# Eighteen places instead of fourteen for the gathered down rows of an expert stage, on one core of a Trainium2

## The chip, the cores and the metric

The kernel runs on one core of a Trainium2 chip. The metric is the device time of one execution in microseconds (us). The kernel before took 2483.57 us, the median of three runs (2480.18 to 2490.12).

A core has four computing engines that run side by side: PE (TensorE, the matrix engine; the profile lists its weight loads apart, as PEld), DVE (VectorE), ACT (ScalarE) and POOL (GpSimd). SP (SyncE) only issues transfers here. Each engine takes its own list of instructions strictly in order, and engines wait for each other by semaphores: an instruction raises a counter when it is done, another waits until the counter has reached a value. DMA engines move data between the device memory and SBUF, the core's working memory; matmuls add up in PSUM.

## The reference

The reference is two blocks of a network on 256 tokens of width 1024, in float32. The part that the change touches is the expert layer of the first block (`peer`). For every token and each of 8 heads it finds 16 experts, takes one row of `peer_u` and one row of `peer_v` for each, and sums up:

```python
q = (xt @ w_pq).reshape(T, PEER_HEADS, 2, PEER_QDIM // 2)
s = jnp.einsum('thpd,hpnd->thpn', q, subkeys).astype(jnp.float32)
top_s, top_i = lax.top_k(s, PEER_TOPK)
...
act = jax.nn.gelu(jnp.einsum('thkd,td->thk', peer_u[eb], xb), approximate=False) * gb
return jnp.einsum('thk,thkd->td', act, peer_v[eb])
```

Both tables have 16384 rows of 1024 numbers. Which rows are wanted is known only when the scores of the token have been sorted, so the rows are gathered by index. Behind this layer come the second block's feed-forward layers and mixers, all of them dense matrix products with streamed weights.

## The kernel before, in words

The kernel is a sequence of stages; in each, every engine has its own list. The stage of interest is `peer_experts` (line 2299). The 256 tokens stand as 2 blocks of 128, one token per partition. A *job* is one head of one block (16 jobs), and each job has 16 *slots*, so there are 256 slots, called rows 0 to 255 below. For row i the engines do this:

- POOL, `gather(i)` (lines 2509 to 2524), issues two indirect DMAs: the u row of 128 tokens (128 x 1024 numbers, 0.52 MB) into one of `U_RING` = 6 places, and the v row ("down row", of the same size) into one of `V_RING` = 14 places. It does so strictly in the order u(0), v(0), u(1), v(1), and so on. Before u(i) it waits until the dot product of row i-6 is done (line 2516).
- DVE (line 2685) multiplies the u row with the tokens and sums it into one number per token, the *dot* of row i. Between the dots DVE sorts scores (`top16`) and works out which experts the next jobs use (`experts_of`) and their gates (`gates_of`), at fixed places of its list. `gates_of(2)` stands ahead of the dot of row 28.
- ACT, `weigh` (lines 2436 to 2450), turns two dots at a time into weights (a gelu, times the gate) and writes each weight on the diagonal of a 128 x 128 matrix. There are `DIAGONALS` = 8 of these matrices, so the diagonal of row i waits until PE has used that of row i-8 (line 2448).
- PE, `weighted_row(i)` (line 2361 on), multiplies that diagonal matrix with the v row in two halves, adding up in PSUM (line 2365), and raises `rows_used` by one.

What the v gather waits for is this (lines 2519 to 2524):

```python
if i >= V_RING:
    pool.wait_ge(S["rows_used"], (i - V_RING) + 1)
elif i >= EARLY_SLOT:
    pool.wait_ge(k.w.used, k.w.early + i - EARLY_SLOT + 1)
```

So rows 0 to 5 wait for nothing. The eight places of rows 6 to 13 (`v_rows_early`) first hold chunks 4 to 11 of the query weights `w_pq`, and row 6+c waits until PE has used chunk 4+c. From row 14 on, row i waits until PE has used row i-14.

The stage begins with the queries: PE computes 16 of them (`queries(n)`, query 0 still in the stage ahead), 1 to 3 from rounded and low parts of the tokens (the pair of tensors `moving_mem`, line 3659, passed as `parts`), 4 to 15 from whole numbers (line 2354). Queries 1 to 11 come ahead of `weighted_row(0)`, 12 to 15 are put between rows 8 and 15. After each query ACT copies it out (line 2425) and PE computes key scores with it (line 2342), which ACT copies out as well (line 2432). ACT's list has all of this and the exponentials of the gates (line 2418); those for `gates_of(2)` come behind the diagonals of rows 16 and 17.

At the end of the stage, block 0 is complete with row 239. ACT copies its sum (`total_out(0)`, line 2483, behind the diagonals of rows 242 and 243), PE transposes it (line 2399, ahead of row 246), DVE adds it to the residual (`add_features(0)`, line 2638) ahead of the dot of row 249. The rest follows behind row 255.

Of the kernel before, what the change touches and what calls it, by code (L numbers as in the profile page):

```python
# [25 lines left out]
D = 1024  # L26
# [9 lines left out]
PEER_HEADS, PEER_KEYS, TOPK = 8, 128, 16  # L36
# [19 lines left out]
SPLIT = 4  # L56
CHUNK = 8 * P
LEVELS = 7
X_SUM = 5
U_RING, V_RING, DIAGONALS = 6, 14, 8  # L60
EARLY_CHUNKS = 8
SPLITS_LEFT = 3

# [1977 lines left out]
def token_mixer(k, mem, mem_parts, parts):  # L2041
    with ExitStack() as ctx:
        sb = lambda name, *shape: k.sbuf(ctx, name, *shape)
        m = {"parts": parts, "spare": mem, "w_ba": sb("w_ba", KT, 8), "rows": sb("gdn_rows", 8),
             "beta": sb("beta", TB, 4), "decay": sb("decay", 3, TB, 4),
             "z": sb("z_silu", 4, T), "squares": sb("squares_and_outputs", 8, T),
             "gates": sb("gates", 16, T), "qkv": sb("qkv", 12, T)}
        m |= {"o_sb": m["squares"][:, 0:4, :], "o_gdn": m["squares"][:, 4:8, :]}
        with ExitStack() as early:
            eb = lambda name, *shape: k.sbuf(early, name, *shape)  # L2050
            m |= {"sb_qk": eb("sb_qk", 8, T), "sb_v": eb("sb_v", TB, 512),
                  "conv_in": eb("conv_in", 12, T + CONV_TAPS - 1), "mem_scale": eb("mem_scale", 2, T)}
            project_in(k, m, mem, mem_parts)
            stick_breaking(k, m)
        gdn_chunks(k, m)
        merged = k.pair(ctx, "merged", KT, T)
        project_residual(k, merged, "g_cross", parts, mem_parts, make=MergedBranches(k, ctx, m, merged))


def cross_attention(k, parts, mem_parts, subkeys):  # L2060

    with ExitStack() as ctx:
        q, kk = k.sbuf(ctx, "xq", KT, T), k.sbuf(ctx, "xk", KT, T)
        v_tok = k.sbuf(ctx, "xv", TB, D)
        project_residual(k, parts, "g_peer", mem_parts, mem_parts, tokens=k.xn, make=CrossHeads(k, ctx, q, kk, v_tok, parts, mem_parts, subkeys))
# [188 lines left out]
def peer(k, parts, subkeys, last_rows):  # L2254


    with ExitStack() as ctx:
        peer_experts(k, ctx, parts, subkeys, last_rows)
# [40 lines left out]
def peer_experts(k, ctx, parts, keys, last_rows):  # L2299

    S, stale = k.stage()
    first = k.w.taken - 1
    N, K = 2 * PEER_HEADS, TOPK
    SLOTS_ALL = JOBS * K
    EARLY_SLOT = V_RING - EARLY_CHUNKS
    SCORES_AT, FIRST, LAST_AHEAD = 2, 8, 12
    sb = lambda name, *shape, dtype=F32: k.sbuf(ctx, name, *shape, dtype=dtype)
    route = Route(k, ctx)
    q, diagonal = sb("peer_q", 2, T), keys
    totals = k.xn[:, :, :].rearrange("p n d -> p (n d)").rearrange("p (b d) -> p b d", b=TB)  # L2310
    dots = sb("expert_dots", SLOTS_ALL)
    gelus, weights = sb("expert_gelus", SLOTS_ALL), sb("expert_weights", SLOTS_ALL)
    u_rows, first_rows = sb("u_rows", U_RING, D), sb("v_rows", EARLY_SLOT, D)
    places = [first_rows[:, s, :] for s in range(EARLY_SLOT)] + [last_rows[:, c, :] for c in range(EARLY_CHUNKS)]
    v_row = lambda i: places[i % V_RING]
    x_squares = route.key_scores
    block_of = lambda i: (i // K) % TB
# [8 lines left out]
    with k.nc.Block() as block:  # L2326
        @block.sync
        def _(sp):
            clear(sp, stale)
            k.w.load_ahead(sp, first, N - RING - SPLIT + len(SPLIT_AT))  # L2330
            last = SLOTS_ALL - 1
            sp.wait_ge(k.v_ready[last % V_RING], 16 * (last // V_RING + 1))
            k.w.load_ahead(sp, first, N - SPLIT + len(SPLIT_AT))
# [173 lines left out]
        @block.gpsimd  # L2507
        def _(pool):
            def gather(i):
                index = bass.IndirectOffsetOnAxis(ap=route.experts[:, i // K, i % K:i % K + 1], axis=0)  # L2510
                if i in (0, FIRST):
                    pool.wait_ge(S["routed"], i // FIRST + 1)
                elif i % K == 0:
                    pool.wait_ge(S["routed"], i // K + 2)
                if i >= U_RING:
                    pool.wait_ge(S["dots"], i - U_RING + 1)
                pool.indirect_dma_start(out=u_rows[:, i % U_RING, :], out_offset=None, in_=k.dram["peer_u"],  # L2517
                                        in_offset=index).then_inc(k.u_ready[i % U_RING], 16)
                if i >= V_RING:
                    pool.wait_ge(S["rows_used"], (i - V_RING) + 1)  # L2520
                elif i >= EARLY_SLOT:
                    pool.wait_ge(k.w.used, k.w.early + i - EARLY_SLOT + 1)
                pool.indirect_dma_start(out=v_row(i), out_offset=None, in_=k.dram["peer_v"],  # L2523
                                        in_offset=index).then_inc(k.v_ready[i % V_RING], 16)

            for i in range(SLOTS_ALL):
                gather(i)
# [410 lines left out]
def nsa_mixer(k):  # L2938

    with ExitStack() as ctx:
        sb = lambda name, *shape: k.sbuf(ctx, name, *shape)
        m = {"q": sb("nsa_q", 4, T), "cmp_in": sb("cmp_in", 2, 2, T), "k_sw": sb("nsa_k", 2, T),
             "v_sw": sb("nsa_v", TB, 2, P), "conv": sb("conv_in2", 12, T), "w_g": sb("w_g", KT, 24),
             "gates": sb("nsa_gates", TB, 24), "cmp": sb("nsa_cmp", NSA_HEADS * TB, 32), "o": sb("nsa_o", KT, T),
             "w1": sb("cmp_w1", 2, CMP_STRIDE, P), "w2": sb("cmp_w2", 2, NSA_DIM), "pos": sb("cmp_pos", 2, CMP_STRIDE),
             "kc": sb("kc", N_CMP), "vc": sb("vc", NSA_REP, P), "parts": k.pair(ctx, "moving", KT, T)}
        project_late(k, "l0_mix_post_g_2", m["parts"], NsaHeads(k, ctx, m), banks=(6, 7, 2, 3))  # L2950
# [703 lines left out]
def build(nc, dram):  # L3654

    with ExitStack() as ctx:
        k = Kernel(nc, ctx, dram)
        with ExitStack() as until_peer:
            mem_parts = k.pair(until_peer, "moving_mem", KT, T)
            with ExitStack() as early:  # L3660
                parts, mem = k.pair(early, "moving", KT, T), k.sbuf(early, "mem", KT, T)
                load_and_norm(k, mem)
                token_mixer(k, mem, mem_parts, parts)
                subkeys = k.sbuf(until_peer, "subkeys", 2 * PEER_HEADS, PEER_KEYS, side="right")
                last_rows = k.sbuf(until_peer, "v_rows_early", EARLY_CHUNKS, D, side="right")
                k.w.early_places = [last_rows[:, c, :] for c in range(EARLY_CHUNKS)]
                cross_attention(k, parts, mem_parts, subkeys)
            peer(k, mem_parts, subkeys, last_rows)
        ffn(k, "l0_ffn1", final="g_final")
        nsa_mixer(k)  # L3670
        ffn(k, "l0_ffn2")
        ffn(k, "l1_ffn1")
        rwkv_mixer(k)
        ffn(k, "l1_ffn2")
        store_output(k)
# [113 lines left out]
```

## Time and profile before

| | |
|---|---|
| median of three runs | 2483.57 us (2480.18 to 2490.12) |
| the profiled execution | 2478.28 us, its span 2476.3 us |
| granted clock of PE, mean over the span | 0.95 |
| PE, PEld, DVE, ACT, POOL busy | 89%, 73%, 65%, 40%, 20% of the span |
| first and last gather of the expert stage | 419.56 and 1163.65 us |
| what is gathered | 268.47 MB of the 509.44 MB that all DMAs move |

The profile is of one execution; its times are counted from the start of its span. An engine's row in a timeline gives start, duration, engine, line, operation, tiles and number of instructions, and in brackets how long the engine had been idle and what ended that. The names that the profile gives to releasers are inferred: where a row says that a DMA from the start of the program (`x_residual<-in_x`) ended a wait, it was something else, and the code has to be asked. The diagonal matrices lie where the keys lay, and appear as `subkeys`.

### The profile page before, as it was taken

The page shows a single profiled execution, that of the slowest core. Times are in us where ns is not written, and L with a number is a line of the kernel's source. Part 1 is how long each engine was busy: PE and PEld are TensorE (multiplying, and loading weights), DVE is VectorE, ACT ScalarE, POOL GpSimd, SP SyncE. Part 2 cuts the span into 40 slices and gives each one's busy share as a digit, 9 for nine tenths or more (in the row PEclk, how much of TensorE's full clock was granted, in tenths as well). Part 3 has the DMA queues.
Part 4 walks back from the last instruction along what each step waited for, and adds up shares of the span by engine and source line. Part 5 has one row for each costly group of instructions (what it writes and reads, how often), then busy time and mean ns, then how long its engine had stood idle before and what let it go on. Part 6 is the DMA issues. An engine that isn't in the chain of part 4 may idle for free. (4 is left out here: it accounts for less than half of the span.)

```text
span 2476.3 us, 40698 instructions
## 1 busy us (share of the span) xinstructions
PE 2201.6 (89%) x15970; PEld 1804.3 (73%) x15970; DVE 1616.7 (65%) x3172; ACT 987.7 (40%) x1894; POOL 503.2 (20%) x532
## 2 busy tenths in 40 slices
PE   8998999897777776767999999999999898999998
PEld 7987988542222322223999997999999777888998
DVE  6676756765566566553766766766766868648666
ACT  5553544243233332322544444444543563014433
POOL 0000001566666666664100000000000000000000
PEclk9999999898898888888999999999999999999999
DMA  5530573899999999998455541555455432002653
GB/s 204 180 96 18 172 254 134 313 355 366 373 371 364 370 371 367 367 384 326 146 183 184 181 128 60 163 182 184 153 184 183 145 94 86 3 3 90 195 184 111
DMA packets 140318, 509.44 MB, mean 206 GB/s; under 512 B 15968, under 2 KB 16608, under 8 KB 139744
## 3 DMA queue, kind: packets, MB, share of 16 engines
q1 hardware_dynamic: 65824, 237.32, 29.8%
q0 software_dynamic: 73728, 268.47, 28.6%
q8 instruction: 128, 2.10, 0.3%
q10 hardware_dynamic: 576, 1.05, 0.1%
q14 instruction: 62, 0.51, 0.1%
HBM read 505.72 MB, written 1.05 MB: 205 GB/s over the span
## 5 line engine op out<-in xcount | busy, mean ns | idle before, releaser
L249 DVE TENSOR_TENSOR weights_low<-weights,weights_high 128x1024 fp32r<-128x1024 f32 x424 | 520.6, 1229 | 284.8 <-ACT weights_high L240 282.7
L240 ACT ACTIVATE weights_high<-weights 128x1024 fp32r<-128x1024 f32 x424 | 446.7, 1058 | 495.0 <-PE ps L285 382.2
L283 PE MATMUL ps<-moving_high,weights_high 128*128 128x256 f32 x2126 | 609.0, 286 | 8.7 <-DVE moving_low L1350 3.8
L285 PE MATMUL ps<-moving_high,weights_low 128*128 128x256 f32 x2126 | 602.9, 284 | 0.0
L284 PE MATMUL ps<-moving_low,weights_high 128*128 128x256 f32 x2126 | 602.9, 284 | 0.0
L2685 DVE CUSTOM_DVE_ANT_0 u_rows<-u_rows,ps 128x1024 f32<-128x1024 f32 x256 | 308.3, 1219 | 236.2 <-DMA u_rows<-in_peer_u,experts 178.0
L2365 PE MATMUL ps<-v_rows_early,subkeys 128*128 128x512 f32 x576 | 305.8, 685 | 137.8 <-issue 123.6
L283 PEld LDWEIGHTS ps<-moving_high,weights_high 128*128 128x128 f32 x2126 | 409.4, 193 | 13.0 <-issue 9.9
L284 PEld LDWEIGHTS ps<-moving_low,weights_high 128*128 128x128 f32 x2126 | 409.3, 193 | 0.2
L285 PEld LDWEIGHTS ps<-moving_high,weights_low 128*128 128x128 f32 x2126 | 409.0, 192 | 0.0
L2365 PEld LDWEIGHTS ps<-v_rows_early,subkeys 128*128 128x128 f32 x576 | 121.3, 218 | 316.1 <-issue 316.0
L2517 POOL DMA_INDIRECT u_rows<-in_peer_u,experts x256 | 241.9, 945 | 457.2 <-DVE experts L2600 372.1
L2365 PE MATMUL ps<-v_rows,subkeys 128*128 128x512 f32 x448 | 210.0, 620 | 40.6 <-issue 36.6
L2365 PEld LDWEIGHTS ps<-v_rows,subkeys 128*128 128x128 f32 x448 | 87.2, 199 | 158.2 <-issue 158.0
L2796 PE MATMUL ps<-hidden_high,weights_high 128*128 128x256 f32 x704 | 199.2, 283 | 0.0
L2796 PE MATMUL ps<-hidden_low,weights_high 128*128 128x256 f32 x704 | 199.2, 283 | 0.0
L2796 PE MATMUL ps<-hidden_high,weights_low 128*128 128x256 f32 x704 | 199.2, 283 | 0.0
L3598 POOL COPY inverse_t<-consts 128x512 f32<-128x512 f32 x8 | 4.6, 614 | 931.9 <-POOLq L3054 872.2
L2449 ACT ACTIVATE subkeys<-consts,expert_weights 128x128 f32<-128x128 f32 x256 | 89.9, 389 | 192.4 <-DMA x_residual<-in_x 136.0
L2523 POOL DMA_INDIRECT v_rows_early<-in_peer_v,experts x144 | 136.7, 949 | 90.2 <-issue 34.7
L2796 PEld LDWEIGHTS ps<-hidden_high,weights_high 128*128 128x128 f32 x704 | 135.2, 192 | 0.0
L2796 PEld LDWEIGHTS ps<-hidden_low,weights_high 128*128 128x128 f32 x704 | 135.2, 192 | 0.0
(600 smaller groups left out, 3417.6 us busy)
## 6 DMA issues: line engine op xcount, KB each, us to landing
weights<-in_l_ffn SPq DMA_DIRECT2D x264, 512.0 KB, 3.6
weights<-in_w_in SPq DMA_DIRECT2D x44, 512.0 KB, 3.7
weights<-in_l_in SPq DMA_DIRECT2D x24, 512.0 KB, 3.6
weights<-in_l_rkv SPq DMA_DIRECT2D x24, 512.0 KB, 3.5
weights<-in_w_ckv SPq DMA_DIRECT2D x16, 512.0 KB, 4.0
weights<-in_w_up_pair SPq DMA_DIRECT2D x8, 512.0 KB, 3.6
weights<-in_w_mix_out SPq DMA_DIRECT2D x8, 512.0 KB, 4.2
weights<-in_w_cq SPq DMA_DIRECT2D x8, 512.0 KB, 5.1
```

The costliest lines, as they stand in the source:

```text
L240: act.activation(self.high[:, c % SPLIT, :], self.source(c), ACT.Copy).then_inc(self.rounded, 1)
L249: v.tensor_tensor(self.low[:, c % SPLIT, :], self.source(c), self.high[:, c % SPLIT, :].bitcast(F32), ALU.subtract).then_inc(self.split, 1)
L283: pe.matmul(out, lhs.high, rhs.high, start=start, stop=False)
L284: pe.matmul(out, lhs.high, rhs.low, start=False, stop=False)
L285: return pe.matmul(out, lhs.low, rhs.high, start=False, stop=stop)
L2365: last = pe.matmul(k.ps[:, sum_bank(tb) + half, :], diagonal[:, i % DIAGONALS, :], v_row(i)[:, 512 * half:512 * half + 512], start=i < TB ...
L2449: act.activation(diagonal[:, n % DIAGONALS, :], k.const("identity"), ACT.Copy, scale=weights[:, n:n + 1])\
L2517: pool.indirect_dma_start(out=u_rows[:, i % U_RING, :], out_offset=None, in_=k.dram["peer_u"], in_offset=index).then_inc(k.u_ready[i % U_R ...
L2523: pool.indirect_dma_start(out=v_row(i), out_offset=None, in_=k.dram["peer_v"], in_offset=index).then_inc(k.v_ready[i % V_RING], 16)
L2685: v.tensor_tensor_reduce(out=row, in0=row, in1=tokens[block_of(i)], scale=1.0, scalar=0.0, op0=ALU.mult, op1=ALU.add, accum_out=dots[:, i: ...
L2796: last = pe.matmul(acc[:, o, :], w[:, o, :], m, start=f == n == 0 and o % 2 == 0, stop=f == FT - 1 and n == 2, skip_group_check=True)
L3598: pool.tensor_copy(u[:, g, :, :], over(k.const("identity"), 4)).then_inc(S["identities"], 1)
```

## The change

`V_RING` goes from 14 to 18, and four of the places (`BORROWED`) are a new tensor of the expert stage, `v_rows_in_parts`. It is the first tensor that the stage allocates, and the pair `moving_mem` is given back just ahead of the stage, so it lies where the tokens' rounded and low parts lay. To make this possible, `subkeys` and `v_rows_early` move to another scope. The four borrowed places are those of rows 6 to 9; each of these waits until PE has used chunk 3 of the query weights, the last product that reads the parts. Rows 10 to 17 wait for chunks 4 to 11, as rows 6 to 13 did, and from row 18 on row i waits until PE has used row i-18. There are 18 semaphores for landed v rows in place of 14, and SP's wait for the last of them follows the new count. Nothing else changes: the number of transfers and of instructions that compute stays.

```diff
-U_RING, V_RING, DIAGONALS = 6, 14, 8
+U_RING, V_RING, BORROWED, DIAGONALS = 6, 18, 4, 8
...
     EARLY_SLOT = V_RING - EARLY_CHUNKS
+    BORROWED_SLOT = EARLY_SLOT - BORROWED
...
+    rows_in_parts = sb("v_rows_in_parts", BORROWED, D)
...
-    u_rows, first_rows = sb("u_rows", U_RING, D), sb("v_rows", EARLY_SLOT, D)
-    places = [first_rows[:, s, :] for s in range(EARLY_SLOT)] + [last_rows[:, c, :] for c in range(EARLY_CHUNKS)]
+    u_rows, first_rows = sb("u_rows", U_RING, D), sb("v_rows", BORROWED_SLOT, D)
+    places = [first_rows[:, s, :] for s in range(BORROWED_SLOT)] + [rows_in_parts[:, s, :] for s in range(BORROWED)]
+    places += [last_rows[:, c, :] for c in range(EARLY_CHUNKS)]
...
                 elif i >= EARLY_SLOT:
                     pool.wait_ge(k.w.used, k.w.early + i - EARLY_SLOT + 1)
+                elif i >= BORROWED_SLOT:
+                    pool.wait_ge(k.w.used, first + SPLIT)
...
-        with ExitStack() as until_peer:
+        with ExitStack() as until_ffn, ExitStack() as until_peer:
...
-                subkeys = k.sbuf(until_peer, "subkeys", 2 * PEER_HEADS, PEER_KEYS, side="right")
-                last_rows = k.sbuf(until_peer, "v_rows_early", EARLY_CHUNKS, D, side="right")
+                subkeys = k.sbuf(until_ffn, "subkeys", 2 * PEER_HEADS, PEER_KEYS, side="right")
+                last_rows = k.sbuf(until_ffn, "v_rows_early", EARLY_CHUNKS, D, side="right")
...
+            until_peer.close()
             peer(k, mem_parts, subkeys, last_rows)
```

## Rows read from the trace of the kernel before

**Rows 1.** Groups of POOL's instructions, 419 to 1166 us: name, shapes, count, busy, mean ns, idle before.

```profile
L2517 POOL DMA_INDIRECT u_rows<-in_peer_u,experts x256 | 241.9, 945 | 457.2 <-DVE experts L2600 372.1 <-issue 74.6 <-DVE expert_dots L2685 10.4
```

**Rows 2.** POOL's timeline: the first gather, one row at full pace, the last gather.

```profile
419.56 1.15 POOL L2517 DMA_INDIRECT u_rows<-in_peer_u,experts  x1 [372.11 <-DVE experts L2600]
...
479.85 0.94 POOL L2523 DMA_INDIRECT v_rows<-in_peer_v,experts  x1 [0.30 <-issue]
481.09 0.94 POOL L2517 DMA_INDIRECT u_rows<-in_peer_u,experts  x1 [0.30 <-issue]
482.33 0.94 POOL L2523 DMA_INDIRECT v_rows<-in_peer_v,experts  x1 [0.30 <-issue]
...
1163.65 0.94 POOL L2523 DMA_INDIRECT v_rows<-in_peer_v,experts  x1 [0.30 <-issue]
```

**Rows 3.** Stretches: length, busy time (instructions) of five engines, PE clock, DMA share, GB/s.

```profile
443.00:470.00 27.00, 26.57 (x122) 22.00 (x121) 20.59 (x75) 11.56 (x38) 11.71 (x14) 0.94 0.74 237
535.00:1165.00 630.00, 454.06 (x906) 185.08 (x905) 361.86 (x825) 191.06 (x607) 415.59 (x440) 0.85 0.97 368
...
557.00:573.00 16.00, 11.63 (x27) 4.67 (x25) 10.80 (x20) 4.44 (x14) 12.04 (x14) 0.98 1.03 410
```

**Rows 4.** POOL's waits for v places, 535 to 1165 us: total, times, longest.

```profile
POOL v_rows L2523 <- DMA x_residual<-in_x: 26.4, 11, 4.2
POOL v_rows_early L2523 <- DMA x_residual<-in_x: 23.6, 10, 4.6
POOL v_rows L2523 <- PE ps L2365: 23.2, 15, 5.1
...
POOL v_rows_early L2523 <- PE ps L2365: 11.5, 11, 3.4
```

**Rows 5.** POOL's timeline: v(8) and v(13), waiting for query chunks, and v(17).

```profile
447.23 0.94 POOL L2523 DMA_INDIRECT v_rows_early<-in_peer_v,experts  x1 [3.88 <-PE ps L2354]
...
467.42 0.94 POOL L2523 DMA_INDIRECT v_rows_early<-in_peer_v,experts  x1 [1.72 <-PE ps L2354]
...
477.36 0.94 POOL L2523 DMA_INDIRECT v_rows<-in_peer_v,experts  x1 [0.30 <-issue]
```

**Rows 6.** DVE's timeline: the gates of job 2 and the dot of row 28; POOL's: u(34).

```profile
521.00 0.16 DVE L2629 RECIPROCAL gate_sum<-gate_sum 128x1 f32<-128x1 f32 x1 [6.42 <-ACT expert_gates L2418]
...
521.34 1.21 DVE L2685 CUSTOM_DVE_ANT_0 u_rows<-u_rows,ps 128x1024 f32<-128x1024 f32 x1
...
530.12 0.94 POOL L2517 DMA_INDIRECT u_rows<-in_peer_u,experts  x1 [0.30 <-issue]
```

**Rows 7.** PE's timeline: rows 34 to 41, and 43; then 44 to 47.

```profile
551.07 13.90 PE L2365 MATMUL ps<-v_rows_early,subkeys 128*128 128x512 f32 x32
...
568.16 1.96 PE L2365 MATMUL ps<-v_rows,subkeys 128*128 128x512 f32 x4 [1.48 <-issue]
578.94 8.91 PE L2365 MATMUL ps<-v_rows,subkeys 128*128 128x512 f32 x16 [8.82 <-issue]
```

**Rows 8.** The same moment on ACT (diagonals 44 and 45) and POOL (v(50), v(61)).

```profile
578.39 0.69 ACT L2449 ACTIVATE subkeys<-consts,expert_weights 128x128 f32<-128x128 f32 x2 [8.73 <-DMA x_residual<-in_x]
...
578.29 0.94 POOL L2523 DMA_INDIRECT v_rows_early<-in_peer_v,experts  x1 [4.65 <-DMA x_residual<-in_x]
...
609.61 0.94 POOL L2523 DMA_INDIRECT v_rows<-in_peer_v,experts  x1 [2.77 <-PE ps L2365]
```

**Rows 9.** The stage's end: PE's rows 238 to 241, ACT's copy of block 0's sum.

```profile
1126.02 7.03 PE L2365 MATMUL ps<-v_rows,subkeys 128*128 128x512 f32 x16
...
1150.40 1.08 ACT L2483 ACTIVATE x_normed<-ps 128x512 f32<-128x512 f32 x2 [16.34 <-DMA x_residual<-in_x]
```

**Rows 10.** POOL's timeline at the end: v(240), v(254), u(255); DVE's block 0 sum.

```profile
1118.71 0.94 POOL L2523 DMA_INDIRECT v_rows<-in_peer_v,experts  x1 [2.77 <-PE ps L2365]
...
1158.37 0.94 POOL L2523 DMA_INDIRECT v_rows<-in_peer_v,experts  x1 [5.14 <-PE ps L2365]
1162.41 0.94 POOL L2517 DMA_INDIRECT u_rows<-in_peer_u,experts  x1 [3.10 <-DVE expert_dots L2685]
...
1159.71 1.28 DVE L2638 TENSOR_TENSOR x_residual<-x_residual,ps 128x512 f32<-128x512 f32 x2 [14.28 <-PE ps L2399]
```

**Rows 11.** PE's last query 5 products, ACT's copy of query 5.

```profile
427.67 2.76 PE L2354 MATMUL ps<-x_normed,v_rows_early 128*128 128x256 f32 x12
...
440.93 0.38 ACT L2425 ACTIVATE peer_q<-ps 128x256 f32<-128x256 f32 x1 [7.68 <-remote]
```

## The prediction

> **What bounds the kernel now.** The change lies in one stage, so I looked first at POOL's groups and waits, then at the stretches, and last at the timelines of all engines around single waits. The stage's gathers run from 419.6 to 1163.65 us [rows 2]: 744.1 us for 256 rows, 2.91 us each. At full pace POOL issues a row's two gathers in 2.48 us (479.85 to 482.33), so POOL alone would need 635 us. A row is 1.049 MB; where the transfers run full they move 410 GB/s [rows 3], which is 2.56 us a row, 655 us in all. The stage is thus paced by its gathers, but stands 89 us above what they need. It is not lost on u places, for which POOL waited 10.4 us in the whole stage [rows 1], but on v places: 26.4 + 23.6 + 23.2 + 11.5 = 84.7 us in 47 waits between 535 and 1165 us [rows 4], of which 0.3 each is the ordinary step between instructions [rows 2], so 70.6 us. Ahead of 535 us there are waits for query chunks, 3.88 us and five of 1.7 to 2.4 [rows 5]; there the transfers fall to 237 GB/s [rows 3].
>
> This looks like an invitation to add places. Whether they help depends on why the place isn't free. The row to look at is v(50): it waits until row 36 is used, till 578.29 us [rows 8]. PE's rows 34 to 41 ran from 551.07 at 1.72 us each [rows 7], so row 36 was through at about 556.2. The count reached POOL 22 us later. ACT waited for the very same count (diagonal 44 wants row 36 used) until 578.39, and PE stood idle for 8.8 us for want of that diagonal. At the stage's end it is seen again: row 239 is through on PE at about 1129.5 (1126.02 and two rows), and ACT, which waits for it, goes on at 1150.40 [rows 9]. So in this stage PE's counts arrive late, by about 20 us, though PE had nothing to do. I read from the two timelines that it happens while the gathers keep the transfers full (410 GB/s in the stretch ahead of 573), and that the counts come once POOL has stopped issuing for a few us: 4.65 us here, 5.14 us at v(254) [rows 10]. That POOL's stop lets the counts through is an inference; the rows show only that they come together.
>
> **The change, part by part.** *Unchanged work.* 512 gathers, 256 dots, diagonals and weighted rows stay; the new tensor, the scopes and four more semaphores issue nothing. SP's wait for the last v row moves to another semaphore, for the same row. No cost: bound 0 on both sides, unless places elsewhere in SBUF move data differently, for which no row gives a reason.
>
> *The start.* Rows 6 to 9 now wait for chunk 3, which was used before query 5's last products began at 427.67 [rows 11], earlier than v(6) is issued. v(7)'s own wait, whose count came late too, I leave as it is. From 441.2 us POOL can run at 2.49 us a row until v(17), which wants chunk 11, as v(13) did: it goes out at 467.4 in place of 477.4 [rows 5], 10.0 us or four rows ahead. This lead is cut at row 34: u(34) needs the dot of row 28, which stands behind the gates of job 2; these come from ACT at 521.0, behind queries 12 to 15 and the diagonals up to row 17, a chain that no gather feeds. The dot ends at 522.5, u(34) was at 530.1 [rows 6]: lead 7.6 us, three rows. Queued behind POOL's waiting u(34) are only later gathers. The fourth row comes back where POOL next meets a v wait, since it may then run four rows further.
>
> *The steady part.* If the reading above holds, four more places let POOL run four rows further into the time in which counts are held back, once. After that POOL stops as before, for 3 to 5 us, and gets as many rows for it as before: the eight that ACT's diagonals allow PE to be ahead of the count, and the three or four that PE gets counted soon after. Now that is 11 rows from v(50) to v(61), 31.3 us [rows 8]. ACT, stopped by the ring of eight diagonals, is not helped by v places at all. So POOL keeps a lead of three to four rows, and the pace of the counts, which PE's and ACT's work follows, stays. Ends for this part: 0 if nothing but the lead remains, 67 us if all waits fall away (first rival). I take 0, by the row where ACT and POOL wait for the same count.
>
> *The end.* What is the lead worth? v(240) went out at 1118.71 [rows 10]; v(244) would in its place, and v(254), ten rows on and with no wait, at 1143.6 in place of 1158.4. Then u(255) waits for the dot of row 249, behind the sum of block 0, which DVE adds at 1159.71. That sum hangs on ACT's copy at 1150.40. POOL now stops at 1144.5; the counts came 4.9 us after its stop at 1153.2, so now at about 1149.4. ACT's copy is 1.0 us earlier, and what follows takes as long as before. So of 10 us only about 1 survives at the tail. Between 1 and 10 us I take 3, near the lower end: 1 from the tail, and 2 because in some of the twenty stretches ACT waits for dots rather than for a count, where the lead serves it.
>
> The sum: 2478.28 - 3 = 2475.3 us for the profiled execution. The median of the runs shown lies 5.3 us above it, so 2483.57 - 3 = 2480.6 us.
>
> There is one page to weigh here. The Trainium skill, "HBM Reference", Specifications, gives about 358 GB/s as the effective rate of one core; by it 268.5 MB would take about 750 us, the stage would already be at its limit, and no number of places could shorten it (estimate: 2483.6 us). The trace disagrees: 410 GB/s over 16 us, and a mean of 368 over 630 us [rows 3]. So the room is there, and this rule does not lower the chance of the rivals that gain.
>
> **The rivals.** *All v waits fall away.* If counts come late by some 20 us whatever POOL does, four places (10 us) cover every single wait of up to 5.1 us, and the transfers become the bound: from v(36) to v(255), 219 rows, 560 us at 2.56 in place of 627. That is -67, about 2416 us. For it: the waits are short and one by one. Against: ACT's ring of eight diagonals waits for the same counts and would stop PE, and in the rows at hand counts came after stops.
>
> *Fewer stops.* Each stop buys 16 rows in place of 12, since the longer lead lets PE work off more when counts flow. The waits of 70.6 us shrink by a quarter, 17.6, and 10 us of lead last to the end: -28, about 2456 us. For it: between stops POOL is what limits. Against: just after a stop PE works without a gap (rows 44 to 47 in one piece [rows 7]), so it has no use for more rows.
>
> *Slower: the query chain is starved of its counts.* Between 443 and 470 POOL now throttles itself, at 237 GB/s; with four rows of lead it would keep the transfers nearly full while PE runs queries 7 to 11. Query 5 shows the price: PE was done with it at about 430.4, and ACT got the count at 440.93 after 7.68 us of idleness, under full transfers [rows 11]. Queries, key scores, rows 0 to 17 and the gates of job 2 are one chain, so each such hold moves the dot of row 28 by 7.7 us. One hold eats the lead of 7.6; two make +7.8; three of the five queries would make +15.5, about 2499 us. It decides from the point at which a query's count comes more than 3.9 us late, the spacing of these waits. Against: POOL is held by the same counts after four rows, and then lets them through.
>
> *The change does nothing* (a lead that no one uses) differs from my forecast by 3 us and is counted in it.
>
> **How the numbers follow.** Forecast 0.60; all waits gone 0.10; fewer stops 0.17; starved queries 0.13. A measurement of this kernel can tell about 0.5%, 12.4 us, from no change. So faster is 0.10 + 0.17 = 0.27, same 0.60, slower 0.13. The range goes from 2452 (with the fewer stops, without the first rival) to 2495 (without the worst of the starved queries, with two holds and 4 us of spread). The forecast's own range is 2471 to 2492.
>
> **What would show it right or wrong.** Right: v(17) near 467.4; u(34) at 522 to 524; in the steady part about twenty stops of 3 to 5 us, with ACT waiting at the same moments, POOL now some ten rather than six rows ahead of ACT's diagonal; 2.85 to 2.91 us a row; v(254) without a wait, POOL stopped at u(255) instead. Wrong: if POOL's v waits beyond 535 us sum to much less than 70 us, or the mean rate of the transfers there rises above 375 GB/s, the reading of the late counts has failed and the kernel is faster; if ACT's idle time ahead of line 2425 grows between 443 and 470 and the gates of job 2 come after 529, it is slower.

## The result, and the profile after

The changed kernel is slower by a little: 2492.48 us against 2486.62 (medians of 20 runs each), ratio 1.0026 with a 95% interval of 1.0016 to 1.0036. Forecast was -3 us; measured is +6.5 by the ratio (0.0026 of 2486.6), +5.9 by the two medians. The profiled execution took 2498.25 us, span 2496.5, so it lies in the upper part of its own runs (2483.7 to 2501.0), and the one of before (2478.28) at the low end of its (2479.1 to 2492.4): of the 20 us between the two traces about 13 are the spread of single executions. Hence I read the traces for what happens, and the medians for what it costs. One of the ten executions of e18 below took 3075.24 us at a granted clock of 0.65 and is left out of its ratio.

POOL's group for the u gathers, and its waits for places from 535 us to the end of the stage. They answer to [rows 1, 4]:

```profile
L2520 POOL DMA_INDIRECT u_rows<-in_peer_u,experts x256 | 243.3, 951 | 480.5 <-DVE experts L2605 372.0 <-issue 76.9 <-DVE expert_dots L2690 31.6
```

```profile
POOL v_rows_early L2528 <- DMA x_residual<-in_x: 27.3, 11, 5.5
POOL v_rows L2528 <- DMA x_residual<-in_x: 19.1, 8, 4.4
POOL v_rows L2528 <- PE ps L2368: 12.2, 7, 3.3
POOL v_rows_in_parts L2528 <- DMA x_residual<-in_x: 11.3, 5, 4.7
POOL v_rows_early L2528 <- PE ps L2368: 5.4, 4, 2.8
POOL v_rows_in_parts L2528 <- PE ps L2368: 3.4, 3, 2.8
```

These sum to 78.7 us in 38 waits (84.7 in 47 before): four more places took away next to nothing of the waits for places. ACT's waits in the same stretch (total, times, longest), first of the kernel after, then of the one before (535 to 1165 us):

```profile
ACT subkeys L2452 <- DMA x_residual<-in_x: 179.5, 35, 10.1
ACT subkeys L2452 <- PE ps L2368: 150.2, 49, 8.1
ACT expert_gelus L2441 <- DVE expert_dots L2690: 20.5, 7, 9.3
```

```profile
ACT expert_gelus L2438 <- issue: 171.8, 46, 9.2
ACT subkeys L2449 <- DMA x_residual<-in_x: 136.0, 25, 8.7
ACT expert_gelus L2438 <- DVE expert_dots L2685: 54.2, 15, 8.1
ACT subkeys L2449 <- PE ps L2365: 39.2, 13, 5.2
```

A wait ahead of `subkeys` is one for a free diagonal, that is for PE's count of row i-8. The DMA of x named in half of these rows was over long ago; the count is what ended them. ACT now waits 330 us for counts where it waited 175, and hardly ever for dots: POOL and DVE are further ahead, and that serves no one. The stretches, answering to [rows 3]:

```profile
443.00:470.00 27.00, 19.22 (x85) 16.32 (x86) 25.23 (x88) 7.15 (x22) 15.04 (x17) 0.80 0.91 323
535.00:1185.00 650.00, 471.16 (x935) 193.09 (x934) 365.91 (x835) 200.13 (x642) 420.94 (x444) 0.85 0.94 357
```

The tail, answering to [rows 10] and the copy of [rows 9]: POOL, then ACT and DVE.

```profile
1165.77 0.94 POOL L2528 DMA_INDIRECT v_rows<-in_peer_v,experts  x1 [1.51 <-issue]
1171.43 0.94 POOL L2528 DMA_INDIRECT v_rows<-in_peer_v,experts  x1 [3.47 <-DMA x_residual<-in_x]
1182.12 0.94 POOL L2520 DMA_INDIRECT u_rows<-in_peer_u,experts  x1 [9.75 <-DVE expert_dots L2690]
```

```profile
1171.37 1.09 ACT L2486 ACTIVATE x_normed<-ps 128x512 f32<-128x512 f32 x2 [5.37 <-PE ps L2368]
...
1179.43 1.28 DVE L2643 TENSOR_TENSOR x_residual<-x_residual,ps 128x512 f32<-128x512 f32 x2 [20.73 <-PE ps L2402]
```

v(253) goes out at 1165.77, v(254) at 1171.43 after a wait where none was foretold, and ACT's copy of block 0's sum starts only at 1171.37, in the same moment as v(254). u(255) then waits 9.75 us (3.10 before) for the dot that stands behind DVE's sum.

### The profile page after: what moved, and what is told of

Same layout as the page of the kernel before. It is cut to its first block and busy times, and to the rows that moved or that the text cites. A ratio compares the mean times of both kernels' runs of the same rounds, so it can differ in the third digit from the quotient of the medians.

```text
span 2496.5 us, 40698 instructions
## 1 busy us (share of the span) xinstructions
PE 2214.1 (89%) x15970; PEld 1813.2 (73%) x15970; DVE 1616.3 (65%) x3172; ACT 988.5 (40%) x1894; POOL 504.4 (20%) x532
## 5 line engine op out<-in xcount | busy, mean ns | idle before, releaser
L2368 PE MATMUL ps<-v_rows_early,subkeys 128*128 128x512 f32 x448 | 225.1, 656 | 81.8 <-issue 56.8
L2368 PEld LDWEIGHTS ps<-v_rows_early,subkeys 128*128 128x128 f32 x448 | 91.8, 210 | 211.9 <-issue 211.8
L2368 PE MATMUL ps<-v_rows,subkeys 128*128 128x512 f32 x352 | 179.1, 663 | 58.9 <-issue 58.2
L2368 PEld LDWEIGHTS ps<-v_rows,subkeys 128*128 128x128 f32 x352 | 72.9, 213 | 160.9 <-issue 160.8
L2368 PE MATMUL ps<-v_rows_in_parts,subkeys 128*128 128x512 f32 x224 | 117.9, 677 | 39.9 <-issue 39.9
```

The lines of the kernel that those rows point to most:

```text
L2368: last = pe.matmul(k.ps[:, sum_bank(tb) + half, :], diagonal[:, i % DIAGONALS, :], v_row(i)[:, 512 * half:512 * half + 512], start=i < TB ...
```

## The experiments

The chips turned out to differ. On some the kernel before takes 2479 to 2488 us, and PE's counts come late as in the traces above (e1 to e4, e13, e14, e17, e18: called late chips here). On others the very same kernel takes 2393 us (e5 to e12, e15, e16: prompt chips). Each ratio is against the kernel before on the same chip.

**Start or steady part?** e1 keeps eighteen places but gives the start its old waits; e2 keeps the new start, but row i waits for row i-14.

```diff
 e1
-                elif i >= EARLY_SLOT:
-                    pool.wait_ge(k.w.used, k.w.early + i - EARLY_SLOT + 1)
+                elif i >= EARLY_SLOT + BORROWED:
+                    pool.wait_ge(S["rows_used"], i - EARLY_SLOT - BORROWED + 1)
                 elif i >= BORROWED_SLOT:
-                    pool.wait_ge(k.w.used, first + SPLIT)
+                    pool.wait_ge(k.w.used, k.w.early + i - BORROWED_SLOT + 1)
 e2
-                    pool.wait_ge(S["rows_used"], (i - V_RING) + 1)
+                    pool.wait_ge(S["rows_used"], i - 14 + 1)
```

> Eighteen places, but the start keeps the waits of the kernel before: v rows 6 to 13 wait for query chunks 4 to 11, rows 14 to 17 for rows 0 to 3; only from row 18 on do the four more places count. Theory 1 (the loss is made at the start: with no wait at rows 6 to 9 the gathers keep the transfers full from 443 to 470 us, PE's counts for the queries come late, and the gates of job 2 move from 521.0 to 533.9): the loss of the changed kernel goes away, ratio to the kernel before 0.998 to 1.000, gates of job 2 near 521. Theory 2 (the loss is made in the steady part: ACT waited 395 us for rows' counts in the changed kernel, 188 before): ratio near 1.0026, the gates of job 2 near 521 all the same.

Measured: 1.0026 (1.0012 to 1.0039).

> The other half alone: rows 6 to 17 wait as in the changed kernel (6 to 9 for chunk 3, 10 to 17 for chunks 4 to 11), but from row 18 on a v row waits for row i-14, as with fourteen places. Theory 1 (loss at the start): ratio to the kernel before 1.002 to 1.005, gates of job 2 near 533. Theory 2 (loss in the steady part): ratio 0.999 to 1.001. If the four places in the steady part are worth the 3 us that the prediction gave them, this one is slower than the changed kernel by about 3 us.

Measured: 1.0004 (0.9989 to 1.0019). Theory 1 has fallen: the loss goes with the four places from row 18 on (e1 and e2 ran on one chip, with medians of 2494.37 and 2488.11 us). It doesn't lie in where the new places are either, since e2 has the very tensors of the changed kernel. The gates of job 2 alone would have misled here. They are shown on DVE, after, e1 and e2 in turn (521.00 before [rows 6]):

```profile
533.60 0.16 DVE L2634 RECIPROCAL gate_sum<-gate_sum 128x1 f32<-128x1 f32 x1 [21.56 <-ACT expert_gates L2421]
```

```profile
531.63 0.16 DVE L2634 RECIPROCAL gate_sum<-gate_sum 128x1 f32<-128x1 f32 x1 [14.08 <-ACT expert_gates L2421]
```

```profile
524.38 0.16 DVE L2634 RECIPROCAL gate_sum<-gate_sum 128x1 f32<-128x1 f32 x1 [5.49 <-ACT expert_gates L2421]
```

They are 10 us late with the old start, against both theories, and 3 late with the new one, so they don't tell the starts apart. The count of query 5 does. These are the traces on late chips, all times in us:

```
start                  old: before     e1      e3      e4   new: after     e2     e13     e18
ACT's copy of query 5       440.93  441.16  439.57  442.72      448.38  449.89  449.52  450.41
v(17)                       477.36  477.46  475.95  479.02      476.73  477.55  477.68  477.17
gates of job 2              521.00  531.63  519.98  524.95      533.60  524.38  534.82  527.65
```

With the new start query 5 reaches ACT 8.5 us later on average, in each of four traces, and v(17) is no earlier for it. In the time of the whole it costs nothing that e2 can show.

**Is the ring of eight diagonals the chain?** e3 is the kernel before with sixteen (the first 16 rows keep eight places, as the others still hold keys):

```diff
-                        act.wait_ge(S["rows_used"], (n - DIAGONALS) + 1)
+                        act.wait_ge(S["rows_used"], n - 8 + 1 if n < 24 else 17 if n < 32 else n - DIAGONALS + 1)
```

> The kernel before with sixteen diagonals in place of eight (the first 16 rows keep eight places, since the others still hold keys), fourteen v places. Theory A (PE's counts are let through only when POOL stops; rows that PE has finished don't bring them sooner): PE no longer waits for diagonals, but POOL's v waits beyond 535 us stay at about 70 us and the ratio is 0.997 to 1.000. Theory B (the ring of eight is the chain: a late count holds the diagonal, that holds PE, and that makes the next count late): v waits halve at least, 2.6 to 2.75 us a row, 30 to 60 us faster, ratio 0.975 to 0.988.

Measured: 0.9997 (0.9984 to 1.0009). ACT's two largest groups of waits in 535 to 1165 us:

```profile
ACT expert_gelus L2439 <- issue: 220.4, 58, 9.2
ACT expert_gelus L2439 <- DVE expert_dots L2686: 183.2, 39, 15.2
```

No wait for a diagonal of more than a step is left on ACT (it still waits 21.9 us for the count of row 239, ahead of its copy), and nothing was won; POOL waited for its fourteen places as before. e13 lengthens both rings:

> The changed kernel (eighteen v places) with sixteen diagonals: both rings that wait for used rows are longer. On a chip where PE's counts come late (kernel before near 2488 us): theory D (every count is late by some 20 us; then either ring alone holds the pace, eight diagonals at (20+3)/8 = 2.9 us a row, fourteen places at (12+8 for the stop+20)/14 = 2.9, and only both together let go): at least 40 us faster, ratio 0.970 to 0.985. Theory A (counts pass only when POOL stops, however long the rings): ratio 0.998 to 1.004. On a chip where they come in time (near 2393 us): ratio 0.998 to 1.001 by both.

Measured on a late chip: 1.0030 (1.0012 to 1.0048). A fixed lateness (theory D) would have let this one go; it has fallen. No length of ring that was tried buys anything: on late chips every kernel with eighteen places lies at 1.0026 to 1.0030 (after, e1, e13, e18), those with fourteen at 0.9997 to 1.0004 (e2, e3, e4).

**Do full transfers hold the counts back, as the prediction had it?** e4 gathers half of each v row:

```diff
-                pool.indirect_dma_start(out=v_row(i), out_offset=None, in_=k.dram["peer_v"],
+                pool.indirect_dma_start(out=v_row(i)[:, 0:512], out_offset=None, in_=k.dram["peer_v"].rearrange("e (h d) -> (e h) d", h=2),
```

> The kernel before with v gathers of half a row (2 KB in place of 4 KB for each of 128 partitions, both products of a row read that half; so the result leaves out half of each v row). POOL issues as many gathers at the same pace, the transfers carry three quarters. Theory A (PE's counts are held back by full transfers): ACT's release after row i-8 comes within 1 us of PE's end of it, no v waits, POOL runs at 2.49 us a row: stage of 640 us in place of 744, whole near 2385 us. Theory B (they are held back by POOL's issuing itself, whatever moves): counts stay 15 to 25 us late, v waits stay, at least 2440 us.

Measured: 1.0000 (0.9982 to 1.0018). Its steady stretch, and a wait like that of [rows 8]: PE's rows 34 to 39, ACT's diagonal 41 and POOL's v(47). Both of these want row 33, which PE had behind it when row 34 began at 555.02:

```profile
535.00:1165.00 630.00, 457.75 (x912) 184.79 (x910) 358.21 (x818) 190.33 (x602) 419.44 (x442) 0.86 0.83 276
...
555.02 10.46 PE L2365 MATMUL ps<-v_rows_early,subkeys 128*128 128x512 f32 x24
...
573.92 0.40 ACT L2449 ACTIVATE subkeys<-consts,expert_weights 128x128 f32<-128x128 f32 x1 [7.30 <-DMA x_residual<-in_x]
...
574.10 0.94 POOL L2523 DMA_INDIRECT v_rows<-in_peer_v,experts  x1 [4.02 <-DMA x_residual<-in_x]
```

At 276 GB/s in place of 368 the counts are as late (19 us here) and the time is the same. POOL issued 442 gathers in these 630 us; 440 before [rows 3].

**Is it the counts themselves?** If few counts get through, one count for four rows should help. The edit is shown for four (e6 and e7); e5 has one for two. e5 and e6 are built on e3, e7 on e13:

```diff
-                last.then_inc(S["rows_used"], 1)
+                if i % 4 == 3:
+                    last.then_inc(S["rows_used"], 1)
```

> Sixteen diagonals and fourteen v places as in e3, but PE counts its used rows once for every two rows. A v row waits for the pair that row i-14 is in, so it has thirteen or fourteen places. Theory C (it is the counts themselves that get through slowly while POOL issues, one in 5 to 10 us, so a count that stands for two rows frees two): the v waits beyond 535 us shrink by half or more, ratio 0.985 or below. Theory D (what comes late is late by a time of some 20 us or until POOL stops, however many rows a count stands for): one place fewer on half the rows, ratio 0.999 to 1.005.

Measured, on a prompt chip: 1.0003 (0.9994 to 1.0013).

> The same with one count for four rows, so eleven to fourteen places. Theory C: four rows for each count that gets through in 5 to 10 us is more than POOL's 2.49 us a row needs; the v waits nearly go, ratio 0.970 to 0.980. Theory D: 1.5 places fewer on average, ratio 1.000 to 1.010.

Measured, prompt chip: 1.0028 (1.0018 to 1.0038).

> The changed kernel (eighteen places, its start) with sixteen diagonals and one count for four rows, so fifteen to eighteen places. Theory C: as e6 or faster, ratio 0.970 to 0.980. Theory D: ratio near the changed kernel's, 1.000 to 1.003.

Measured, prompt chip: 0.9991 (0.9977 to 1.0005). None of the three can tell, since there was no lateness to cure. The question had to wait for e11, e15 and e18, the same kernel:

> e7 once more, wanted on a chip with late counts, where theories C and D of e5 stand apart: C (counts get through slowly, so one count for four rows frees four places): ratio 0.96 to 0.98; D (late by a time, or until POOL stops): ratio 1.000 to 1.005. Where counts come in time, as in e7, neither moves it: 0.998 to 1.001.

Prompt chip again: 0.9994 (0.9983 to 1.0005).

> e7 and e11 once more, wanted on a chip with late counts (kernel before near 2480 us), where e13, its neighbour with a count for every row, took 1.003. Theory C (a stop of POOL lets some eleven counts through, whatever each stands for): stops only every 40 rows or so, ratio 0.970 to 0.980. Theory D/A (a stop lets through what PE has done by then, and counts are held again at once, so it is rows and gathers that are limited, not counts): ratio 1.002 to 1.010. Without late counts: 0.998 to 1.001, as in e7 and e11.

Prompt chip: 0.9996 (0.9986 to 1.0005).

> The kernel of e7, e11 and e15 once more, wanted on a chip with late counts; there, theory C (a stop lets some eleven counts through, whatever each stands for): stops only every 40 rows or so, ratio 0.970 to 0.980; theory B (POOL's issuing holds the counts, so that after each 22 gathers or so POOL has to stop, whatever a count stands for): ratio 1.002 to 1.010, a stop every 11 rows. Where counts come in time: 0.999 to 1.001.

Late chip at last: 1.0029 (1.0008 to 1.0049), as e13 with a count for every row. Theory C has fallen. Theory B has the time right, and nearly the stops: in the trace POOL stands still for more than 1.5 us 22 times from 535 us on, every 21 gathers on average (25 times, every 18, before), but for v places only about every 16 rows, and for dots in between.

**The change on a prompt chip, and a POOL that rests at every row.** e9 is the changed kernel; e10 is the kernel before with `pool.wait_ge(S["dots"], i - 3 + 1)` ahead of u(i).

> The changed kernel once more. The chips differ: where e1 to e4 ran, the kernel before took 2488 us and PE's counts came in bursts after POOL's stops; where e5 to e8 ran it took 2393 us, no count came in a burst, and POOL waited 12.5 us in all for v places. Theory E (the four places cost time only where counts come late, since there POOL runs further ahead before it stops): ratio 1.001 to 1.004 where the kernel before takes some 2488 us, 0.998 to 1.001 where it takes some 2393 us. Theory F (they cost time everywhere): 1.001 to 1.004 on either.

Measured on a prompt chip: 0.9992 (0.9982 to 1.0001): no loss there, so theory E. Its steady stretch and POOL's three largest groups of waits in it (none for v places is longer than the ordinary step of 0.3 us):

```profile
535.00:1060.00 525.00, 399.21 (x828) 161.09 (x826) 338.21 (x782) 173.01 (x556) 384.25 (x408) 0.93 1.03 409
```

```profile
POOL u_rows L2520 <- issue: 46.1, 151, 0.3
POOL u_rows L2520 <- DVE expert_dots L2690: 32.6, 53, 3.3
POOL v_rows_early L2528 <- issue: 21.1, 69, 0.3
```

> The kernel before, but u(i) waits for the dot of row i-3 in place of i-6, so POOL is never more than three rows ahead of the dots and rests a little at every row. On a chip with late counts: theory G (counts pass in any rest of POOL, however short): no bursts, the long v waits vanish, 2.7 to 2.8 us a row, ratio 0.98 to 0.99. Theory H (they pass only some 2.5 to 5 us after POOL's last gather): bursts and v waits stay, ratio 1.00 to 1.02. On a chip without late counts both give a dearer loop: ratio 1.00 to 1.05.

Measured on a prompt chip: 1.0212 (1.0195 to 1.0229), the dearer loop; on a late chip it wasn't tried, so theories G and H stay open.

**Is it the number of gathers?** e8, e12 and e14 (one kernel) fetch v rows for even rows only, from row 14 on: nearly the bytes of e4, three gathers for two rows. The gather's part of the edit:

```diff
+                if i >= V_RING and i % 2:
+                    return
                 if i >= V_RING:
-                    pool.wait_ge(S["rows_used"], (i - V_RING) + 1)
+                    pool.wait_ge(S["rows_used"], (i - V_RING) + 2)
```

> The kernel before with a v gather only for even rows (and for the first 14); PE multiplies an odd row's diagonal with the v row before it, so the result leaves out half of the v rows. POOL issues three gathers for two rows in place of four; the bytes are those of e4, where nothing changed. If each gather that POOL issues holds the counts back (theory B of e4, by number): POOL needs 1.87 us a row and its stops come less often, the stage shrinks by 60 us or more, ratio at most 0.976. If the counts' delay doesn't depend on how many gathers are issued: POOL reaches its last free place sooner and stops longer, and the time is the kernel's before within 0.5%.

Prompt chip: 0.9431 (0.9408 to 0.9455).

> e8 once more (v rows gathered for even rows only, half of them left out of the result), wanted on a chip with late counts. Theory B (each gather that POOL issues holds them back): the stage shrinks from 744 us to 600 or less, ratio 0.93 to 0.95. Theory D (late by some 20 us whatever is issued, with fourteen places that then span 14 rows of which half need one): ratio 0.96 to 1.00. Where counts come in time: 0.943 as in e8.

Prompt chip: 0.9408 (0.9389 to 0.9427).

> e8 once more (v rows gathered for even rows only, half of them left out of the result). On a chip with late counts: theory A/B (counts pass only in POOL's stops, each gather holds them back): time some 0.94 of the kernel before or less. Theory D (a lateness of 20 us that doesn't ask for POOL): the ring of eight diagonals alone keeps 2.8 to 2.9 us a row, time within 1% of the kernel before. On a chip without: 0.94.

Late chip: 2331.91 us, one run, so without an interval, against a median of 2479.94: 0.940, 148 us less, where e4 won nothing. The packets and MB of the gathers' queue, first of e4, then of e14, are nearly the same, so neither bytes nor packets can be what counts:

```profile
q0 software_dynamic: 57344, 201.36, 24.6%
```

```profile
q0 software_dynamic: 56304, 205.02, 23.6%
```

The steady stretch of e14:

```profile
535.00:1010.00 475.00, 407.42 (x894) 172.14 (x892) 349.56 (x812) 186.51 (x591) 309.73 (x325) 0.95 0.96 360
```

POOL issued 325 gathers in 475 us, 0.68 a us. Before it was 440 in 630, 0.70; e4 442; e3, in the same 630 us, 438; e13 442; e18 440; after 444 in 650, 0.68. On the prompt chip e9 issued 408 in 525, 0.78. So in none of these traces of late chips did POOL issue more than 0.70 gathers a us over the stretch, with 2 or 4 KB a partition and with any of the rings. Whether it is their number or the time that POOL spends on each (0.94 us) isn't told apart.

**A version from that.** e16 and e17 put u and v rows of an expert side by side in one table and fetch both with one gather; twelve places of 8 KB (the memory of eighteen v and six u rows), sixteen diagonals. The gather waits for a free place by PE's count alone; the wait for a dot goes. The main lines of the edit:

```diff
-                pool.indirect_dma_start(out=u_rows[:, i % U_RING, :], out_offset=None, in_=k.dram["peer_u"],
-                                        in_offset=index).then_inc(k.u_ready[i % U_RING], 16)
...
-                pool.indirect_dma_start(out=v_row(i), out_offset=None, in_=k.dram["peer_v"],
-                                        in_offset=index).then_inc(k.v_ready[i % V_RING], 16)
+                pool.indirect_dma_start(out=both_rows(i), out_offset=None, in_=k.dram["peer_uv"],
+                                        in_offset=index).then_inc(k.v_ready[i % V_RING], 16)
...
-    out["peer_u"], out["peer_v"] = first["peer_u"], first["peer_v"]
+    out["peer_uv"] = np.concatenate([first["peer_u"], first["peer_v"]], axis=1)
```

> Eighteen v places and sixteen diagonals of e13, but the u and v rows of an expert lie side by side in one table (arranged before the launch, as the other weights are), and POOL fetches both with one gather: 256 gathers of 8 KB a partition in place of 512 of 4 KB, into twelve places for both rows. Nothing is left out. Theory B (counts are held by the number of gathers that POOL issues, some 22 between two stops, as in e13 and e14): on a chip with late counts the stops come only every 22 rows or go away, the transfers bound the stage at 2.56 us a row: 40 to 90 us faster, ratio 0.965 to 0.985. If it is the time under gathers that counts, not their number (rows and stops every 31 us as before): ratio 0.99 to 1.01. Without late counts the transfers bound the stage already: 0.995 to 1.005.

Measured on a prompt chip: 2380.51 us, 0.9944 (0.9927 to 0.9960).

> e16 once more, wanted on a chip with late counts (kernel before near 2480 us). Theory B (the number of gathers that POOL issues holds the counts): the stops come at most every 22 rows, 40 to 90 us faster, ratio 0.965 to 0.985. If it is time under gathers, not their number: stops every 31 us as before, ratio 0.985 to 1.005. Where counts come in time: 0.9944 as in e16.

Measured on a late chip: 2387.42 us against 2487.85, 0.9598 (0.9578 to 0.9618). It beats both kernels on both kinds of chip, and the late chip is now nearly as quick as the prompt one. Its steady stretch on the late chip; ACT's only wait of more than a step; POOL's two largest groups:

```profile
535.00:1060.00 525.00, 400.95 (x845) 163.62 (x844) 349.01 (x802) 179.46 (x575) 199.23 (x212) 0.95 1.01 421
```

```profile
ACT expert_gelus L2443 <- DVE expert_dots L2688: 340.3, 104, 8.0
...
POOL uv_rows L2526 <- PE ps L2370: 169.8, 100, 8.1
POOL v_rows_early L2526 <- PE ps L2370: 114.3, 69, 8.1
```

The transfers run at 421 GB/s without a break, 1.049 MB in 2.49 us, and POOL issues 0.40 gathers a us and waits for places most of the time, which costs nothing, since the transfers are the bound. The counts are no longer late: a gather that waits for row i-12 starts 0.3 us behind PE's end of that row on average, and never more than 2.0 us (192 waits beyond 535 us), where the same measure is 22 us in the kernel before. Full transfers with prompt counts, on a late chip, are what the prediction's reading ruled out. e17 also gives the u rows twelve places for six; before, POOL waited only 10.4 us for u places [rows 1], so that is an unlikely source of 100 us, though no run takes it alone. The Trainium skill ("DMA: Bandwidth & Descriptors", Measured) advises to batch DMAs to 1 MiB and more; this case agrees as far as it goes, with 421 GB/s for gathers of 1.049 MB against 409 for gathers half as large. The rule is about the rate, and most of the gain on a late chip comes from somewhere else: 100 us there, 13 on a prompt one.

## Why the prediction was wrong

**What held.** Counts come late, more places don't shorten the waits beyond 535 us (about 70 us foretold; 78.7 less 0.3 for each of 38 is 67.3), POOL and ACT wait for the same counts, 2.88 us a row from v(40) to v(240) (2.85 to 2.91 foretold), a mean rate of 357 GB/s (under 375). The second rival (fewer stops) would have had fewer and not longer waits; they are fewer (38 for 47) and longer (2.1 us for 1.8). What the first rival foretold, no v waits and the transfers as the bound, is seen on prompt chips alone, and there it comes with the chip and not with the places: 2393.26 us with fourteen, 2391.49 with eighteen (e9).

**The cause of the lateness** was read wrongly. "It happens while the gathers keep the transfers full" has fallen with e4 (276 GB/s, as late) and e17 (421 GB/s, not late). What holds the pace on a late chip is the number of gathers, or the time that POOL spends on them, by e4 against e14 and by e17. A stop of POOL isn't needed for a count to come either: of ACT's waits of more than 1 us for a diagonal (rows 60 to 249), 9 of 32 ended while POOL was issuing before, and 52 of 77 after. The pace of the steady part came out right all the same, and by luck, because either reading has it set elsewhere than by the places.

**The start.** v(17) was to go out at 467.4; it went at 476.73, and u(34) at 535.43 in place of 522 to 524. This is the third rival's mechanism: v(7) waited 2.66 us before and not at all now, and query 5's count, which ACT had at 440.93, came at 448.38 (8.46 us idle). All four traces with the new start on late chips have this hold, and in all four it uses up the lead of 10 us by v(17), which waits for chunk 11 and so for query 11. The term that failed is the query chain, which the sum took as "a chain that no gather feeds", with the hold left to a rival at 0.13; why the count comes later is not shown. On prompt chips the lead at v(17) is 3.0 us (465.01 in e9, 467.98 with fourteen places in e5). The loss of that rival did not follow: e2 shows that the new start costs nothing that 0.15% could show. So the lead of 7.6 us is not there, and no loss either.

**The steady part: the lead.** "POOL keeps a lead of three to four rows" failed. If the counts' pace were given and POOL ran four rows further, v(240) would be out some 10 us sooner. On late chips it went out at 1118.7, 1126.4, 1121.3 and 1123.5 us with fourteen places (before, e2, e3, e4), and at 1127.7, 1127.4, 1121.7 and 1127.5 with eighteen (after, e1, e13, e18). POOL does stand further ahead of the others: when v(i) goes out (rows 60 to 239), ACT's diagonals are 6.9 rows behind on average and PE 9.5, against 3.8 and 5.8 before. But it is POOL that has the given pace; the longer ring makes ACT and PE stand further behind it, and not POOL earlier.

**The end** is the step that most likely turned the sign: "ACT's copy is 1.0 us earlier, and what follows takes as long as before". It hung the copy on POOL's stop, and the kernel before speaks against that: from v(240) at 1118.71 [rows 10] on POOL issued without a pause beyond the ordinary step until 1153.23, and the count of row 239 reached ACT at 1150.40, in the middle of it. POOL around that moment, before:

```profile
1149.81 0.94 POOL L2517 DMA_INDIRECT u_rows<-in_peer_u,experts  x1 [0.31 <-issue]
1151.05 0.94 POOL L2523 DMA_INDIRECT v_rows<-in_peer_v,experts  x1 [0.30 <-issue]
```

So a POOL that stops sooner is no reason for an earlier copy. What the places do change is the order. With fourteen places v(253) waits for the count of row 239, the same that ACT's copy waits for, so the copy is never later than v(253) by more than a moment. With eighteen, v(253) needs row 235 only. Worked out from the traces:

```
places                      14: before    e2     e3     e4   18: after    e1    e13    e18
copy minus v(253), us          -0.7   -14.1   -0.2  -14.6       5.6    5.9   -0.8    7.8
dot 249 minus v(253), us        9.9     9.2    9.3    8.0      14.9   15.4    9.2   16.9
```

The dot of row 249 (behind DVE's sum of block 0) lets u(255) go, and from its start to the end of the span it is 1311 to 1319 us in all eight. It stands 9.1 us behind v(253) on average with fourteen places and 14.1 with eighteen: +5.0 us, the term that I had at -1. The spans of the eight traces differ by 7.2 us on average: 3.6 by v(240), nothing from there to v(253), the 5.0, and -1.4 behind the dot. The 3.6 lie within what executions with fourteen places differ by themselves (1118.7 to 1126.4); the 5.0 are the part that stands out, in three of four traces. In e13 the copy came in time and the execution was quick, 2481.21 us, the lowest of its nine runs. This is read from eight traces of one execution each; no experiment takes the tail alone, so it is the likeliest account, not one that is shown. Shown by e1, e2, e13 and e18 is only that the loss comes with the four places from row 18 on, on late chips. On the prompt chip e9 has the copy 10.4 us ahead of v(253) with eighteen places, and no loss.

## What to carry to other kernels

If an engine waits for a free place, ask first whether the signal or the place is late: another waiter for the same count, and a producer that stands idle, tell that a longer ring will not help. A longer ring can also take away a wait that kept another engine's work in time, so look at the end of the stage, where the lead must be given back. Where POOL issues row gathers back to back, fewer and larger ones come first, places after: one table and one gather for both rows of an expert was worth 4.0% on a late chip and 0.6% on a prompt one, and no longer ring that was tried was worth anything.

## What the runs showed of the hardware

The same program takes 2479 to 2488 us on some chips and 2393 on others, and the traces have nearly all of the difference in the stage in which POOL issues gathers (v(253) of e9 at 1071.7 us, of the kernel before at 1151.0; from dot 249 to the end 1316.6 and 1315.4). PE's granted clock in the steady stretch is lower where counts are late (0.85 before, 0.93 in e9), but e17 has 0.95 on a late chip, so a lower clock isn't what makes a chip late. A comparison should be made on one chip.

On a late chip PE's counts are late, and those of ACT and DVE that could be timed are not. A gelu on ACT that waits for DVE's dot starts within 0.04 us of the dot's end, and PE starts a row 0.14 us behind the end of ACT's diagonal, in the same microseconds in which a count of PE takes 20 us. It isn't one semaphore: DVE's wait for PE's transposes has it too. In e2, PE's transposes and, 13 us later, DVE's sum:

```profile
1156.96 1.04 PE L2402 MATMUL ps<-consts,x_normed 128*128 128x128 f32 x8
...
1171.41 1.29 DVE L2643 TENSOR_TENSOR x_residual<-x_residual,ps 128x512 f32<-128x512 f32 x2 [13.66 <-remote]
```

What in the chip ties PE's counts to the gathers that POOL issues stays open; the runs show the tie and its price, some 1.45 us for each gather of the stage (744.1 us for 512), against 1.28 on a prompt chip (655.8 us, e9), where the transfers are the bound.
